# Two weight tiles that multiply rounded, unnormed rows behind each norm of a two-block transformer kernel

## What is computed

```python
def rms_norm(x, gain):
    y = x * lax.rsqrt(jnp.mean(x * x, axis=-1, keepdims=True) + RMS_EPS)
    return y * gain
for l in range(2):
    proj = rms_norm(h, norm_mix[l]) @ w_in[l]        # 1024 -> some 3,350 columns
    h = h + concat(hgrn2(...), nsa(...)) @ w_out[l]
    h = h + (silu(g) * u) @ w_ffn_out[l]              # g, u = rms_norm(h, norm_ffn[l]) @ w_ffn_in[l]
# second block: the same with g_mix, g_cross (queries of the cross attention), g_mem, g_ffn (routed)
```

## Time and profile before

| | |
|---|---|
| times of three runs | 2604.94 us median, 2602.77 to 2613.46 |
| span of the profiled execution | 2603.8 us, 36897 instructions |
| mean granted TensorE clock | 0.980 |
| busy: TensorE, its weight loads, VectorE, ScalarE, GpSimd | 93%, 67%, 44%, 25%, 43% |
| chain that ended last | TensorE 70%, DMA 14%, VectorE 9%, issue 3% |

### The profile page before, as it was taken

How to read it: one execution, slowest core, us unless ns; L and a number is a source line. 1 busy time by engine, 2 the same in 40 slices (tenths; PEclk the granted TensorE clock), 3 DMA queues, 4 the chain that set the end, 5 groups by cost and what they waited for, 6 DMA issues and landing times.

```text
span 2603.8 us, 36897 instructions
## 1 busy us (share of the span) xinstructions
PE 2413.5 (93%) x12948; PEld 1747.1 (67%) x12948; DVE 1142.4 (44%) x1992; ACT 662.1 (25%) x1286; POOL 1125.9 (43%) x766
## 2 busy tenths in 40 slices
PE   7999899999998999899999999999999798887884
PEld 5778667888886778678888877777686533333331
DVE  5676685112346675764112354434565621111113
ACT  4332572111003424562111011124513300000001
POOL 4772206666766762106666765553164011111111
PEclk9999999999999999999999999999999899999998
DMA  3213102333322213003333322221135399999996
GB/s 141 66 49 98 33 10 88 94 96 97 95 89 74 71 49 98 25 10 97 97 97 97 124 81 81 81 89 49 49 96 198 122 386 404 408 403 401 410 408 271
DMA packets 78173, 373.29 MB, mean 143 GB/s; under 512 B 11232, under 2 KB 11360, under 8 KB 53344
## 3 DMA queue, kind: packets, MB, share of 16 engines
q1 hardware_dynamic: 71904, 360.09, 38.8%
q0 software_dynamic: 5280, 8.40, 1.0%
q10 hardware_dynamic: 864, 3.15, 0.3%
HBM read 367.92 MB, written 12.58 MB: 146 GB/s over the span
## 4 chain that ended last, share of the span: by engine, by line
PE 70%; DMA 14%; DVE 9%; issue 3%; ACT 2%; POOL 2%; SPq 0%; DVEq 0%; POOLq 0%; ACTq 0%
PE PS L2042 16%; PE PS L2044 16%; PE PS L2043 16%; DMA arena<-w_up 13%; PE PS L2716 4%; PE PS L2429 2%; PE PS L2458 2%; PE PS L2169 1%; PE PS L2743 1%; PE PS L2443 1%; PE PS L2406 1%; PE PS L2103 1%; PE PS L2049 1%; PE PS L2120 1%; PE PS L2521 1%
## 5 line engine op out<-in xcount | busy, mean ns | idle before, releaser
L596 POOL TENSOR_SCALAR whi<-ring 128x1024 fp32r<-128x1024 f32 x256 | 295.5, 1154 | 930.4 <-PE PS L2044 735.0
L599 POOL TENSOR_TENSOR wlo<-ring,whi 128x1024 fp32r<-128x1024 f32 x256 | 648.9, 2535 | 21.3
L2042 PE MATMUL PS<-xh,whi 128*128 128x512 f32 x1312 | 524.0, 399 | 17.6 <-POOL wlo L599 6.9
L2043 PE MATMUL PS<-xl,whi 128*128 128x512 f32 x1376 | 539.5, 392 | 0.0
L2044 PE MATMUL PS<-xh,wlo 128*128 128x512 f32 x1312 | 513.8, 392 | 0.0
L2716 PE MATMUL PS<-arena,xraw 128*64 128x512 f32 x512 | 244.5, 626 | 73.8 <-DMA arena<-w_up 68.8
L2042 PEld LDWEIGHTS PS<-xh,whi 128*128 128x128 f32 x1312 | 247.9, 189 | 77.7 <-issue 13.6
L2043 PEld LDWEIGHTS PS<-xl,whi 128*128 128x128 f32 x1376 | 260.7, 189 | 53.0 <-issue 2.9
L2044 PEld LDWEIGHTS PS<-xh,wlo 128*128 128x128 f32 x1312 | 247.8, 189 | 52.9
L2717 PE MATMUL PS<-arena,xraw 128*64 128x512 f32 x512 | 245.8, 629 | 0.0
L2716 PEld LDWEIGHTS PS<-arena,xraw 128*64 128x64 f32 x512 | 68.9, 143 | 214.0 <-issue 208.4
(11 more groups left out here) (492 smaller groups left out, 4131.6 us busy)
## 6 DMA issues: line engine op xcount, KB each, us to landing
ring<-ring_w SPq DMA_DIRECT2D x280, 512.0 KB, 3.6
arena<-w_gate SPq DMA_DIRECT2D x64, 1024.0 KB, 25.2
arena<-w_up SPq DMA_DIRECT2D x64, 1024.0 KB, 27.3
xraw<-w_down SPq DMA_DIRECT2D x32, 1024.0 KB, 28.9
arena<-w_down SPq DMA_DIRECT2D x30, 1024.0 KB, 29.0
arena<-y_dram SPq DMA_DIRECT2D x8, 512.0 KB, 6.9
xT<-xT_in SPq DMA_DIRECT2D x2, 1024.0 KB, 6.9
out<-arena SPq DMA_DIRECT2D x4, 512.0 KB, 2.6
```

The lines of the kernel that those rows point to most:

```text
L596: nc.gpsimd.tensor_scalar(hi, ring[:, t % RING, :], 1.0, 0.0, ALU.mult, ALU.add).then_inc(sems["whi"], 1)
L599: nc.gpsimd.tensor_tensor(wlo[:, t % RING, :], ring[:, t % RING, :], hi, ALU.subtract).then_inc(sems["split"], 1)
L2042: mm(out, a[0], b[0], start=start, stop=False, skip_group_check=skip_group_check)
L2043: mm(out, a[0], b[1], start=False, stop=False, skip_group_check=skip_group_check)
```

## The change

The first two tiles behind the mixer norms, the second block's first norm and the cross norm multiply rows that have only been multiplied by the gain and rounded. For the first three, ScalarE makes high parts `rh` beside the squares and VectorE low parts `rl` (`raw_lows`), in the arena; VectorE multiplies the two products by rstd as it takes them from PSUM (`raw_tile`). The normed rows `xh`, `xl` are still made, for all tiles from 2 on. For the cross norm `xh` and `xl` themselves are the unnormed rows, as both its tiles are served by them. TensorE's order at a norm is `behind_norm`. High parts of more weight tiles go to spare buffers, so that the tiles behind a norm can be split before the last ones of the stage are used: `split` has a parameter `back` for the tile it waits for. The fillers at the norms go. The start loads the first weight tile ahead of the second half of x. `PE_STEPS` is written anew. The G and U weights of an expert share one semaphore.

```diff
+        spare = [arena_r[:, o:o + 1024] for o in (6144, 7168, 9728)]
+        rh, rl = (arena_r[:, o:o + KO * T].rearrange("p (a b) -> p a b", b=T) for o in (12288, 16384))
...
-            def split(base, t, second=None):
+            def split(base, t, second=None, back=2):
...
-                if second is None:
-                    pool.wait_ge(sems["tile"], base + (t - 1 + RING))
+                if second is None and back:
+                    pool.wait_ge(sems["tile"], base + (t + 1 - back + RING))
...
+            for t in range(3):
+                split(0, t, spare[2] if t == 2 else None, back=0)
             with pool.Fori(0, DEPTH) as l:
                 base = l * T_LAYER
-                for t in range(T_FFI):
+                for t in range(3, T_FFI):
...
                 for t in range(T_LAYER - 4, T_LAYER):
-                    split(base, t, whi_last if t == T_LAYER - 1 else None)
+                    split(base, t, spare[t - (T_LAYER - 2)] if t >= T_LAYER - 2 else None)
+                split(base, T_LAYER, back=4)
+                split(base, T_LAYER + 1, back=4)
+                pool.wait_ge(sems["xs"], l * FFC + FFC)
+                split(base, T_LAYER + 2, spare[2])
...
+            def raw_norm(l):
+                ln_exp_tables()
+                act_e.wait_ge(sems["params"], nth("params", l, 1))
+                for c in range(KO):
+                    act_e.wait_ge(sems["h"], nth("h", l, c + 1 - 8))
+                    nc.scalar.activation(rh[:, c, :], xT[:, c, :], ACT.Identity, scale=lcol[:, C_MIX + c:C_MIX + c + 1]
+                                         ).then_inc(sems["rh"], 1)
+                    nc.scalar.activation(sqe[:, c, :], xT[:, c, :], ACT.Square).then_inc(sems["sq"], 1)
+                mean_rstd(l, 0, 4)
+                for c in range(KO):
+                    act_e.wait_ge(sems["xr"], nth("xr", l, c + 1))
+                    nc.scalar.activation(xh[:, c, :], xr[:, c, :], ACT.Identity).then_inc(sems["xh"], 1)
...
-                if t < 4:
+                if t < 2:
+                    act_e.wait_ge(sems["raw"], nth("raw", l, t + 1))
+                    ins = nc.scalar.activation(kT[:, t, :], kT[:, t, :], ACT.Sigmoid)
+                elif t < 4:
                     ins = nc.scalar.activation(kT[:, t, :], src, ACT.Sigmoid)
...
+            def raw_lows(l):
+                for c in range(KO):
+                    v.wait_ge(sems["rh"], nth("rh", l, c + 1))
+                    nc.vector.scalar_tensor_tensor(out=rl[:, c, :], in0=xT[:, c, :], scalar=lcol[:, C_MIX + c:C_MIX + c + 1],
+                                                   in1=rh[:, c, :], op0=ALU.mult, op1=ALU.subtract
+                                                   ).then_inc(sems["rl"], 1)
+            def raw_tile(l, i, dst, scale=1.0):
+                v.wait_ge(sems["tile"], nth("tile", l, i + 1))
+                nc.vector.scalar_tensor_tensor(out=dst, in0=PS[:, i, :], scalar=scale, in1=rstd, op0=ALU.mult,
+                                               op1=ALU.mult).then_inc(sems["raw"], 1)
...
+                    raw_tile(l, 0, kT[:, 0, :])
                     low_parts(l, i)
+                    raw_tile(l, 1, kT[:, 1, :])
...
                     residual(l, lambda l, c: chunk_done(l, 4, T_FFO + FFC, c), sums=(l + 1, 0, 0))
+                    raw_lows(l + 1)
...
+            def behind_norm(l, t, n, j, high, low):
+                high_parts(l, PS[:, 0, :], t, *high)
+                mean_square(l, n, j, bank=4)
+                high_parts(l, PS[:, 1, :], t + 1, *high)
+                low_part(l, PS[:, 0, :], t, *low)
+                low_part(l, PS[:, 1, :], t + 1, *low)
...
 PE_STEPS = steps(
-    "norm0 feat0 feat1 feat2 feat3 feat4 feat5 feat6 feat7 feat8 gram0 gram1 feat9 gram2 gram3 feat10 "
-    "feat11 feat12 rs0 gram4 gram5 feat13 gram6 gram7 feat14 feat15 rs1 rs2 rr0 feat16 gram8 gram9 rr1 rs3 "
-    "gram10 gram11 feat17 rr2 feat18 feat19 gatem0 gram12 rr3 gram13 rs4 gram14 gram15 rs5 hi0 rr4 hi1 hi2 "
+    "norm0 feat2 feat3 feat4 feat5 feat6 feat7 feat8 feat9 gram0 gram1 feat10 gram2 gram3 feat11 "
+    "feat12 rs0 feat13 gram4 gram5 feat14 gram6 gram7 feat15 rs1 rs2 rr0 feat16 feat17 gram8 gram9 rr1 rs3 "
+    "gram10 gram11 feat18 rr2 feat19 gatem0 gram12 rr3 gram13 rs4 gram14 gram15 rs5 hi0 rr4 hi1 hi2 "
```

More of the change, by code:

```diff
@@ L90 @@
     sq=16, sqsum=2, rstd=2, xr=8, xh=16, xn=16,
+    rh=8, rl=8, raw=2,
     xs=FFC, xsh=FFC, wh=4, wl=4, wadd=6, wpart=4,
@@ L510, in load_tiles @@
                         sp.dma_start(ring[:, s, :], ring_w[i * RING + s]).then_inc(slot[s], 16)
-            load_tiles(0, RING)
+            for t in range(1, RING):
+                sp.wait_ge(sems["tile"], t + 1)
+                sp.dma_start(ring[:, t, :], ring_w[t]).then_inc(slot[t], 16)
             sp.dma_start(misc_all[:, :, :], misc_in).then_inc(s_in, 16)
@@ L652, in _ @@
                     split(j * 4 + DEPTH * T_LAYER, B_AB + u)
-            with pool.Fori(0, 2) as j:
-                for u in range(4):
-                    split(j * 4 + DEPTH * T_LAYER, B_WO + 4 + u, whi_last if u == 3 else None)
+            for t in range(B_WO + 4, B_CO + 2):
+                if B_WO + 6 <= t < B_CQ:
+                    split(DEPTH * T_LAYER, t, spare[t - (B_WO + 6)])
+                elif t < B_CQ or t == B_CO:
+                    split(DEPTH * T_LAYER, t)
+                elif t < B_CO:
+                    split(DEPTH * T_LAYER, t, back=4)
+                else:
+                    split(DEPTH * T_LAYER, t, spare[0])
             def first_gather(u):
@@ L749, in late_norm @@
                     nc.scalar.activation(sq8[:, c, :], xT[:, c, :], ACT.Square).then_inc(sems["sq"], 1)
[L750 to L753, removed]
+                mean_rstd(l, 1, 4)
             ch = {"base": 0, "n": 0}
@@ L911, in step2 @@
                 l = DEPTH
-                if kind == "norm":
-                    norm_rstd(l, *NORMS2[i], mem=i == 1, sqe=xn if i == 3 else sqe)
+                if kind == "norm" and i == 0:
+                    raw_norm(l)
+                elif kind == "norm" and i == 2:
+                    cross_norm(l)
+                elif kind == "norm":
+                    norm_rstd(l, *NORMS2[i], mem=i == 1, sqe=xn)
                 elif kind == "msq":
@@ L924, in step2 @@
                     nc.scalar.activation(small[:, 0:2], small[:, 0:2], ACT.Exp).then_inc(sems["act_once"], 1)
-                elif kind == "feat":
+                elif kind == "feat" and i < 2:
+                    act_e.wait_ge(sems["raw"], nth("raw", l, i + 1))
+                    act_e.sem_inc(sems["evac"], 1)
+                elif kind == "feat" and i < 16:
                     act_e.wait_ge(sems["tile"], nth("tile", l, tile2_of(i) + 1))
@@ L1539, in residual @@
                     nc.vector.tensor_tensor(xT[:, c, :], xT[:, c, :], PS[:, c, :], ALU.add).then_inc(sems["h"], 1)
-                    if late and c >= 2:
+                    if late and not sums and c >= 2:
                         low(c - 2)
@@ L1544, in residual @@
                 if late:
-                    low(6)
-                    low(7)
+                    for c in range(0 if sums else 6, KO):
+                        low(c)
             def add_part(l, c, bank):
@@ L1753, in _ @@
                 add_squares(0, 0, 0, c)
+            raw_lows(0)
             assert ch["n"] == V_FIRST, ch["n"]
@@ L2078, in step @@
                     pe.wait_ge(sems["evac"], nth("evac", l, i - 1))
[L2079 removed]
+                    feature_major(l, PS[:, i % 2, :], t, 0 if i == 2 else None, hi=spare[2] if i == 2 else None
+                                  ).then_inc(sems["tile"], 1)
                 elif kind == "hi":
@@ L2273, in step @@
                         kouter(l, T_FFO + k, T_FFO + k, k, False, False)
-                    kouter_pair(l, T_FFO + FFC - 2, FFC - 2, False, whi_last)
-                    mean_square(l + 1, 0, 1, done=nth("h", l, 9))
+                    kouter_pair(l, T_FFO + FFC - 2, FFC - 2, False, spare[0:2])
             def step2(kind, i):
```

132 lines of the change are left out of this document (82 added, 50 removed).

## The result

The changed kernel takes 2645.67 us (median of four runs, 2643.86 to 2655.41), the kernel before 2606.14 beside it (four runs, 2602.77 to 2613.46): a ratio of 1.0162 (1.0152 by the two medians alone) with a 95% interval of 1.0149 to 1.0175. Predicted were 2649 us in a range of 2616 to 2668. The profiled execution has a span of 2642.0, 38.2 us more than before.

A forecast was written before the change was run, and what follows sets the result against it. TensorE, busy for 93% of the span, was taken as nearly full, with each head's chain just covered by feature tiles. Two layers 53.0 + 2.4 - 1.6 - 9.3 = + 44.5 us on the median 2604.9: 2649, range 2616 to 2668.

The forecast's parts named there:

- tile 7 later: Each layer, behind the norm: last decay at 824.0 against 822.7, so tile 7 starts 1.3 us later (bounds 3 earlier, 6 later).
- tile 7 to gram 3: Each layer: tiles 9 and 10 both come ahead of gram 3's end, + 5.3 us on 25.1.
- gram 3 to gram 7: Each layer: tile 13, now asked for before gram 4, waits for its split behind `decayed`; 40.9 against 32.2 us, + 8.7.
- gram 7 to gram 11: Each layer: head 2's chain, then the split, then tile 17; 40.4 against 29.2 us, + 11.2.
- behind gram 11: Each layer, after gram 11: order the same and the chain of 15.4 us to tile 19 sets it, 0.
- (1): TensorE at a norm: fillers go, tiles 0 and 1 end 8.8 us earlier, if tile 2 can start.
- (2): VectorE at the norm: added `raw_lows` and `raw_tile`, two meetings with splits; gates start at 808.5 instead of 799.87.
- (3): ScalarE's unchanged order behind the norm: evacuation 1 ends at 811.9, last decay at 824.0 against 822.7, tile 7 1.3 us later.
- (4): Layers: feature tiles moved ahead of grams 0, 2, 4, 6, 8 cost 5.3, 8.7 and 11.2 us per layer.
- (5): Earlier splits into spare buffers meet VectorE's last low part of the streamed rows: 0.8 us three times, + 2.4.
- (6): Second block's norm: no reordering, TensorE the bound behind it; - 1.6 us (bounds + 1 and - 6).
- (7): Cross attention norm: raw rows serve as the only rows, no `xr` or second conversion; - 9.3 us (bounds - 5, - 11).

The follow-up runs named there:

- the run with evacuation 1 first: Changed kernel with TensorE's old order and ScalarE's evacuation 1 ahead of the logarithm of gate 0: 2604.60 us, ratio 0.9997 to the kernel before.
- the old-order row: Stage times of the changed kernel with only TensorE's old order put back: layer 1 783.7, layer 2 766.6 us; whole kernel 2599.05 us.
- The version without fillers and with the raw waits: Changed kernel, old TensorE order, evacuation 1 first, tiles 2 and 3 waiting for VectorE's raw copies, no 12 fillers ahead of tile 8: 2593.43 us, ratio 0.9949.

## Why the prediction was right, point by point

The time came out 3 us below the forecast, but some terms carried each other. Per layer, first and second, from the profiled executions, each step up to the end of what it names (tile 7: to its start):

| step of the prediction | predicted | layer 1 | layer 2 |
|---|---|---|---|
| tile 7 later | + 1.3 | + 1.4 | - 1.7 |
| tile 7 to gram 3 | + 5.3 | + 3.8 | + 6.0 |
| gram 3 to gram 7 | + 8.7 | + 8.6 | + 8.6 |
| gram 7 to gram 11 | + 11.2 | + 13.0 | + 13.2 |
| behind gram 11 | 0 | - 3.7 | - 3.7 |
| rest of the layer | + 0.8 | + 1.7 | + 1.5 |

That the sum is this near is in part luck: the slower pace of the matmuls that read xs, in no term, and the 3.7 us won behind gram 11, put at nothing, cancel.

**(1), (2), (3), the norm.** Fillers gone, tiles 2 and 3 waiting (4.24 and 2.26 us), VectorE meeting two splits: as predicted. On the old scale the low parts of the unnormed rows end at 792.0 (predicted 793), the scaled rows at 797.3 (801.4), and the gates start at 806.8 (808.5). The second meeting fell on the low parts of the normed rows (7.29 us for 4.9) and not on the scaled rows (5.38), and cost 2.4 us, not 3.4. The sum has the end of `raw_lows` right, but that is not their price: without them VectorE would have waited for rstd, which is ready 2.1 us before they end (ScalarE's L784, done at 814.75). From evacuation 1 to the last decay it took 9 us, not 12.1 (one meeting, not nearly two), so the last decay comes at 819.4 where I had 824.0, and tile 7 was at the early side in layer 2. For layer 1 I had only taken the same sum over; that + 1.4 stands beside + 1.3 there is luck as far as the runs tell. That a lead of TensorE would bring the meetings back is what the run with evacuation 1 first shows.

**(4), the order.** The mechanism, the size and the sign are shown by two opposite runs: - 46.6 us when the order is taken out (2645.67 to 2599.05, with the kernel before at 2606.14 and 2604.31 beside them), + 50.8 when it is put in alone.

Tile 7 to gram 3: one tile more, as predicted. But tile 7 itself took 5.7 us and not 7.4, and in layer 2 tile 9 waits 1.87 us for ScalarE.

Gram 3 to gram 7: tile 13 starts 24.5 us behind gram 3, released by its split, where I had 24.4. It names tile 12 among the places of idle time, but has no term for what holds it: ScalarE's queue, which alone would put tile 13 at 23.5. So the idle time stands in front of tile 12 (5.87 us) and not of tile 13 (0.66), and the slower clock falls on tile 12 (8.51 us from start to end, at a granted clock of 0.65) and not on tile 13 (5.72 where I had 7.1). Four fillers ahead of gram 4, 1.0 us, were not in my sum either; these two errors cancel in part, and 8.7 came out as 8.6. Taking the split out of the way won 1 us there (40.8 to 39.8), not the whole.

Gram 7 to gram 11: tile 17 starts 27.1 us behind gram 7 in both layers, released by its split, where I had 23.1 + 4.2 = 27.3. The 3.50 us in which TensorE waits for a rope rstd before that lie inside it. The 2 us more come behind its start: eight fillers ahead of gram 8, which my sum lacks, and tile 17 at 7.5 us where I had 7.1:

```profile
966.66 1.89 PE L2133 MATMUL PS<-mats 128*128 128x256 f32 x8
```

"Behind gram 11 the order is the same" was wrong: tile 17 is multiplied before gram 8 now, and there is less left: tile 19 starts 10.9 us behind gram 11, no longer 15.4, and takes 0.9 more: - 3.7.

**(5), early splits.** Predicted + 2.4 in all, with the low part of the last streamed rows late. The reverse: the idle time in front of the last output tile went from 1.3 us to 0.28 at each of the three places. In the kernel before the conversion of the last rows takes 2.44 us beside the low part of the last split; in the changed one that split is made earlier and the conversion takes 0.71 (read from the traces, not tried by itself). - 3.2 in all. The conversion and the wait behind it, before and after:

```profile
768.68 2.44 DVE L1387 CAST xs<-arena 128x512 fp32r x1 [3.58 <-PE PS L2044]
771.91 0.50 PE L2042 MATMUL PS<-xs,arena_r 128*128 128x512 f32 x1 [1.34 <-DVE xs L1389]
```

```profile
794.51 0.71 DVE L1461 CAST xs<-arena 128x512 fp32r x1 [1.83 <-PE PS L2128]
796.73 0.50 PE L2126 MATMUL PS<-xs,arena_r 128*128 128x512 f32 x1 [0.28 <-DVE xs L1463]
```

**(6), (7).** Second block - 1.4, where - 1.6 and 0.8 of (5) were predicted; cross attention - 8.9 for - 9.3.

**Left out.** The pace of the matmuls that read xs, some 3.3 us a layer; 7.1 us in all by the run that moves xs in the kernel before. Nothing in the trace of before could show it; the table of columns with its new row could have been a term.

So the order costs about 47 us in the layers (profiled executions: 47.5 when taken out, 46.5 when put in; by the medians of the whole kernel 47 and 51). The pace of the matmuls that read xs costs about 7, if it is worth in the changed kernel what it is worth in the one before. The new norms, the first layer's start and the earlier splits among them, then give back 15 to 18: 8.9 at the cross attention, 1.4 in the second block, and net of the pace some 5 in layer 2 and 1 in layer 1 (the old-order row of the table above). The version without fillers and with the raw waits is faster than both kernels, 0.5% under the one before, part of it by the fillers. What remains open is which property of the place counts, and whether it is that of xs.

## What to carry to other kernels

A hand-written order is a balance between queues: before moving work ahead on one engine, list what each of the others has queued in front of what the moved step will wait for, and move those too or leave it. A stage gained by starting TensorE earlier can be lost again if its progress releases another engine's work beside a dense chain that it slows (16.6 us in place of 8.1 here). Before naming the queue that costs the time, look for a second one that ends just before it: here taking away the last gate alone won 1 us of 8.6. When a buffer's size changes, compare the pace of a gap-free stretch before and after.

## What the runs showed that I had not expected

In a gap-free stretch, matmuls of 128x512 whose moving operand had moved by 32 bytes, with the buffers behind it, started 86 times in 20 us and no longer 88 times, at the same granted clock (0.233 us apart, not 0.227).

Two executions of nearly the same kernel (without fillers, and that with xs moved) differ by 5 us in the same stretch of layer 2, from the last Gram products to the mean square of the FFN norm. The granted clock was 0.91 in the one and 0.99 in the other:

```profile
957.30:1037.40 80.10, 77.59 (x471) 68.09 (x469) 45.40 (x70) 26.31 (x44) 19.96 (x12) 0.91 0.29 87
```

```profile
956.50:1031.40 74.90, 72.02 (x474) 63.36 (x473) 48.87 (x71) 26.39 (x44) 20.45 (x12) 0.99 0.30 95
```

A difference of 2 to 3 us between single profiled executions is therefore read as an effect here only where the granted clock of the two stretches agrees or a second layer or run repeats it; otherwise the timed medians are.
